# Index scores as two stacked fp32r passes, block 0 ranked by what it drops, a ranking round before the additions

## What is computed

```python
isc = relu(einsum('bqhd,bkd->bqhk', iq_block, ik))     # scores, 8 heads
isc = einsum('bqhk,bqh->bqk', isc, iw_block)           # weighted sum over heads
isc = where(allowed, isc, NEG)                         # keys of later chunks of 64 are not allowed
_, sel = top_k(isc, topk)                              # topk = 128
```

## Time and profile before

| what | value |
|---|---|
| median of three runs | 1713.42 us |
| the profiled execution | 1714.06 us, its span 1712.2 us |
| PE busy over the span | 1683.4 us, 98% |
| the projection's part of the span | up to about 233.5 us |
| PE in 12.0 to 232.3 us | 216.82 of 220.30 us |
| DVE / ACT / POOL in the same | 149.75 / 79.35 / 100.04 us |

### The profile page before, as it was taken

The page is one execution under the profiler, slowest core; times in us unless marked ns, Lnnn a source line. Parts: engine busy times, 40 slices in busy tenths (PEclk is TensorE's granted clock), DMA queues, the critical chain, the costliest instruction groups (busy, mean ns, idle before and its releaser), DMA issues.

```text
span 1712.2 us, 23324 instructions
## 1 busy us (share of the span) xinstructions
PE 1683.4 (98%) x7786; PEld 1381.9 (81%) x7786; DVE 1091.5 (64%) x2933; ACT 581.6 (34%) x916; POOL 937.8 (55%) x875
## 2 busy tenths in 40 slices
PE   9999999999999999999999999999999999999997
PEld 7877777788888888888888888888888888888886
DVE  4259966456788854444444444434788888888886
ACT  4333227243323222222222222224333333333333
POOL 2744415004433037777777777762777677767710
PEclk9999999999999999999999999999999999999999
DMA  5322142026669554444447444455999999999991
GB/s 177 106 62 62 50 88 62 15 99 222 240 231 315 162 154 143 142 146 147 148 155 235 147 141 144 146 162 190 387 390 369 370 371 363 376 374 368 362 331 49
DMA packets 182673, 351.03 MB, mean 205 GB/s; under 512 B 35600, under 2 KB 118928, under 8 KB 182448
## 3 DMA queue, kind: packets, MB, share of 16 engines
q1 hardware_dynamic: 117824, 255.47, 44.6%
q0 software_dynamic: 34816, 67.41, 11.0%
q10 hardware_dynamic: 29952, 27.28, 4.8%
HBM read 289.04 MB, written 61.02 MB: 204 GB/s over the span
## 4 chain that ended last, share of the span: by engine, by line
PE 74%; DVE 1%; DMA 1%; SPq 1%; POOL 0%; ACT 0%; issue 0%; DVEq 0%; POOLq 0%
PE psum L243 25%; PE psum L244 24%; PE psum L245 24%; DMA ts_raw_wq<-in_peer_wq 1%; PE psum L1735 1%; SPq L1700 0%; POOL ts_lo_wq L1578 0%; SPq L1567 0%; DVE ts_lo_u L1578 0%; POOL ts_lo_u L1578 0%; DVE hit L1867 0%; DVE mixed L2142 0%; DVE mixed L2119 0%; ACT ts_hi_wq L1573 0%; ACT ts_hi_u L1573 0%
## 5 line engine op out<-in xcount | busy, mean ns | idle before, releaser
L2336 POOL DMA_INDIRECT gate_map<-gate_total,gate_at x384 | 403.5, 1051 | 200.9 <-DVE same_expert L2073 110.2
L243 PE MATMUL psum<-x_hi,ts_hi_u 128*128 128x512 f32 x1024 | 399.1, 390 | 2.4 <-POOL ts_lo_u L1578 1.8
L244 PE MATMUL psum<-x_lo,ts_hi_u 128*128 128x512 f32 x1024 | 398.4, 389 | 0.0
L245 PE MATMUL psum<-x_hi,ts_lo_u 128*128 128x512 f32 x1024 | 398.4, 389 | 0.0
L1578 DVE TENSOR_TENSOR ts_lo_u<-ts_raw_u,ts_hi_u 128x1024 fp32r<-128x1024 f32 x116 | 142.2, 1226 | 336.6 <-ACT ts_hi_u L1573 336.6
L245 PE MATMUL psum<-v_hi,c_lo 128*128 128x512 f32 x768 | 298.8, 389 | 0.0
L243 PE MATMUL psum<-v_hi,c_hi 128*128 128x512 f32 x768 | 298.8, 389 | 0.0
L244 PE MATMUL psum<-v_lo,c_hi 128*128 128x512 f32 x768 | 298.8, 389 | 0.0
L1573 ACT ACTIVATE ts_hi_u<-ts_raw_u 128x1024 fp32r<-128x1024 f32 x128 | 135.4, 1058 | 395.0 <-PE psum L245 395.0
L2236 ACT ACTIVATE v_hi<-v_raw 128x1024 fp32r<-128x1024 f32 x128 | 135.8, 1061 | 313.8 <-PE psum L245 310.9
L243 PEld LDWEIGHTS psum<-x_hi,ts_hi_u 128*128 128x128 f32 x1024 | 192.2, 188 | 42.8 <-POOL ts_lo_u L1578 1.9
(11 more groups left out here) (264 smaller groups left out, 2296.0 us busy)
## 6 DMA issues: line engine op xcount, KB each, us to landing
ts_raw_u<-in_peer_u SPq DMA_DIRECT2D x128, 512.0 KB, 3.6
v_raw<-in_peer_v SPq DMA_DIRECT2D x128, 512.0 KB, 5.9
gate_map<-zeros SPq DMA_DIRECT2D x32, 768.0 KB, 6.5
act_in<-up_acts SPq DMA_DIRECT2D x128, 192.0 KB, 6.3
gate_in<-gate_map SPq DMA_DIRECT2D x128, 192.0 KB, 6.6
up_acts<-ut_out_u ACTq DMA_DIRECT2D x104, 192.0 KB, 1.9
raw_in<-in_w_in SPq DMA_DIRECT2D x56, 256.0 KB, 2.8
ts_raw_wq<-in_peer_wq SPq DMA_DIRECT2D x16, 512.0 KB, 6.5
```

What stands on the lines that cost most here:

```text
L243: nc.tensor.matmul(out, l_hi, r_hi, start=first, stop=False)
L244: nc.tensor.matmul(out, l_hi, r_lo, start=False, stop=False)
L245: return nc.tensor.matmul(out, l_lo, r_hi, start=False, stop=last)
L2336: nc.gpsimd.indirect_dma_start(gate_cells, bass.IndirectOffsetOnAxis(places["gate_at"][:, b, j:j + 1], 0), dn.total[:, b, j:j + 1], None). ...
```

## The change

1. **Index queries.** `iq_t` (fp32, two heads stacked) is replaced by `iq_a` and `iq_b` (four heads each, fp32r). Partitions 0 to 63 hold the high part of a head's 64 values, partitions 64 to 127 the low part of the same values. To get both, the rotated tile is written twice, once by POOL and once by DVE, side by side for each head (`rot_twice`, now in `mixed[:, 2 + n % 2]`), so a turn has 8 transposes into two banks. ACT copies both banks with rounding, then DVE subtracts the rounded values from PSUM in the lower half (`low_turned`).
2. **Index keys.** `ik_hi` holds the high part on both halves, `ik_lo` the low part on 64 partitions. A score is one fp32r pass on 128 rows (high and low query parts with the high keys) and one on 64 rows (high query part with the low keys).
3. **Waits.** The turn of rotated output n waits for `idx_lo_done` of n - 2 (n = 2 to 10); an `iq` turn waits for DVE's copy too; DVE's copy of n waits for the turn of n - 2.
4. **Block 0** is ranked by its 16 lowest keys: its weights `iw` are negated, its sums lie reversed in another part of its row, and 2 rounds find the 16 to leave out. The planner then has 50 rounds.
5. **A round first.** On DVE the first round of an output stands before the first two additions, if it ranks a block that is not being added.

```diff
-    iq_t = sb("iq_t", [P, IDX_HEADS // 2, FRAMES], c=c)
-    ik_t = sb("ik_t", [P, ROWS], c=c)
+    iq_a = sb("iq_a", [P, IDX_HEADS // 2, FRAMES], F32R, c=c)
+    iq_b = st["iq_b"]
+    ik_hi = sb("ik_hi", [P, ROWS], F32R, c=c)
+    ik_lo = st["ik_lo"][0:IDX_DIM]
...
+    IQ_BANKS = (4, 6)
+    DROPPED = key_width(0) - TOPK
+    def rounds_of(b):
+        return ROUNDS if b else DROPPED // 8
+    def rounds_ahead(i):
+        scored = [x for j, (x, _, _) in enumerate(items) if items_at(i) and j >= items_at(i)[0]]
+        return sum(order[q] not in scored for q, _ in rounds_at[i][:1])
+    SPLIT_TURNS = sum(name in ("iq", "misc") for _, name, _ in outs)
...
             # PE, turn
+                if 2 <= n < SPLIT_TURNS + 2:
+                    pe.wait_ge(idx_lo_done, n - 1)
+                if name == "iq":
+                    pe.wait_ge(rot_copied, n + 1)
+                    if n == 1:
+                        pe.wait_ge(mt_done, 1)
+                    for x in range(2):
+                        for t in range(4):
+                            last = nc.tensor.transpose(psum[:, IQ_BANKS[x] + n % 2, t * P:(t + 1) * P],
+                                                       rot_twice(n)[:, 4 * x + t].rearrange("p t d -> p (t d)"), ident[:])
+                    last.then_inc(rot_turned, 1)
+                    return
...
             # PE, index_scores
-                s = slice(IDX_DIM * (h % 2), IDX_DIM * (h % 2) + IDX_DIM)
-                nc.tensor.matmul(psum[:, 6 + j % 2, 0:w], iq_t[s, h // 2, b * P:(b + 1) * P],
-                                 ik_t[s, x * w:(x + 1) * w], start=True, stop=True).then_inc(idx_scored, 1)
+                parts = (iq_a, iq_b)[h // 4][:, h % 4, b * P:(b + 1) * P]
+                cols = slice(x * w, (x + 1) * w)
+                nc.tensor.matmul(psum[:, 6 + j % 2, 0:w], parts, ik_hi[:, cols], start=True, stop=False)
+                nc.tensor.matmul(psum[:, 6 + j % 2, 0:w], parts[0:IDX_DIM], ik_lo[:, cols], start=False, stop=True).then_inc(idx_scored, 1)
...
         # DVE, end of dve_rotate
+            if name == "iq":
+                dve.wait_ge(cos_done, n + 1)
+                if n >= 2:
+                    dve.wait_ge(rot_turned, n - 1)
+                nc.vector.tensor_tensor(rot_twice(n)[:, :, 1], by_head(t_cos, n), by_head(t_sin, n), ALU.add).then_inc(rot_copied, 1)
+        def low_turned(dve, i):
+            n = nrot[i]
+            _, name, b = outs[i]
+            dve.wait_ge(turned_copied, n + 1)
+            if name == "misc":
+                r, col = rows(b), META + b * P if b < NB else 0
+                last = nc.vector.tensor_tensor(ik_lo[:, col:col + r], psum[0:IDX_DIM, 4 + n % 2, P:P + r],
+                                               ik_hi[0:IDX_DIM, col:col + r].bitcast(F32), ALU.subtract)
+            else:
+                for x, dst in enumerate((iq_a, iq_b)):
+                    part = dst[IDX_DIM:P, :, b * P:(b + 1) * P]
+                    last = nc.vector.tensor_tensor(part, psum[IDX_DIM:P, IQ_BANKS[x] + n % 2, :].rearrange("p (h n) -> p h n", n=P),
+                                                   part.bitcast(F32), ALU.subtract)
+            last.then_inc(idx_lo_done, 1)
...
         # DVE, loop over outputs
             for i in range(len(outs)):
                 if i in nrot:
                     dve_rotate(dve, i)
+                for t in turns_after(i):
+                    if t in rotated[:SPLIT_TURNS]:
+                        low_turned(dve, t)
...
+                early = rounds_ahead(i)
+                for q, t in rounds_at[i][:early]:
+                    dve_round(dve, q, t)
                 for j in items_at(i)[:2]:
                     dve_add(dve, j)
-                for q, t in rounds_at[i]:
+                for q, t in rounds_at[i][early:]:
                     dve_round(dve, q, t)
...
         # POOL
+                elif name == "iq":
+                    nc.gpsimd.tensor_tensor(rot_twice(n)[:, :, 0], by_head(t_cos, n), by_head(t_sin, n), ALU.add).then_inc(rot_done, 1)
...
         # ACT, copy_turned
+                if name == "iq":
+                    for x, dst in enumerate((iq_a, iq_b)):
+                        last = nc.scalar.activation(dst[:, :, b * P:(b + 1) * P],
+                                                    psum[:, IQ_BANKS[x] + n % 2, :].rearrange("p (h n) -> p h n", n=P), ACT.Copy)
+                    last.then_inc(turned_copied, 1)
+                    return
```

More of the change, by code:

```diff
@@ L151, in program @@
             stream = ExitStack()
+            with ExitStack() as over_rq_t:
+                ik_lo = sb_high("ik_lo", [P, ROWS], F32R, c=over_rq_t)
             ret = dict(
@@ L161, in program @@
                 bias=sb("sel_bias", [P, NB, ROWS], c=stream),
-                gate=sb("gate", [P, NB, 512], c=stream),
+                ik_lo=ik_lo,
             )
+            with ExitStack() as over_gate:
+                st["iq_b"] = sb("iq_b", [P, IDX_HEADS // 2, FRAMES], F32R, c=over_gate)
+            st["gate"] = sb("gate", [P, NB, 512], c=stream)
             st.update(rq_t=ret["rq_t"], rk_t=ret["rk_t"], rv=ret["rv"])
@@ L391, in project @@
     turned_copied = sem("turned_copied")
+    idx_lo_done = sem("idx_lo_done")
+    rot_copied = sem("rot_copied")
+    IQ_BANKS = (4, 6)
     copied = sem("plain_copied")
@@ L408, in project, with ranked, placed @@
     ROUNDS = TOPK // 8
+    DROPPED = key_width(0) - TOPK
+    assert DROPPED % 8 == 0 and 0 < DROPPED < TOPK and order[-1] == 0
+    def rounds_of(b):
+        return ROUNDS if b else DROPPED // 8
+    def ranked(b):
+        w = key_width(b)
+        return bias[:, b, 0:w] if b else bias[:, 0, w:2 * w]
+    def placed(b, cols):
+        return ranked(b)[:, cols] if b else ranked(0)[:, ::-1][:, cols]
     ITEMS = 4
@@ L424, in project @@
     room = [0 if i < first_round or i + 1 == len(outs) else 2 if i in nrot else 3 for i in range(len(outs))]
-    work = sum(ROUNDS * cost(b) for b in range(NB))
+    work = sum(rounds_of(b) * cost(b) for b in range(NB))
     rounds_at, done, at = [[] for _ in outs], 0, first_round
     for q, b in enumerate(order):
-        for t in range(ROUNDS):
+        for t in range(rounds_of(b)):
             while done * sum(room) >= sum(room[:at + 1]) * work:
@@ L432, in project @@
             done += cost(b)
+    def rounds_ahead(i):
+        scored = [x for j, (x, _, _) in enumerate(items) if items_at(i) and j >= items_at(i)[0]]
+        return sum(order[q] not in scored for q, _ in rounds_at[i][:1])
+    SPLIT_TURNS = sum(name in ("iq", "misc") for _, name, _ in outs)
+    assert all(outs[i][1] in ("iq", "misc") for i in rotated[:SPLIT_TURNS])
     def rows(b):
@@ L631, in dve_round @@
             w = key_width(b)
-            r = bias[:, b, 0:w]
-            unseen = bias[0:CHUNK, b, w - CHUNK:w]
+            r = ranked(b)
+            unseen = placed(b, slice(w - CHUNK, w))[0:CHUNK]
             if t == 0:
                 dve.wait_ge(idx_added, max(j for j, it in enumerate(items) if it[0] == b) + 1)
-                nc.vector.memset(unseen, NEG).then_inc(masked_off, 1)
+                nc.vector.memset(unseen, NEG if b else -NEG).then_inc(masked_off, 1)
                 dve.wait_ge(masked_off, 2 * q + 1)
@@ L753, in copy_turned @@
                 else:
-                    tile, h0 = {"iq": (iq_t, 0), "dq0": (st["dq_t"], 0), "dq1": (st["dq_t"], 4), "rq": (st["rq_t"], 0)}[name]
+                    tile, h0 = {"dq0": (st["dq_t"], 0), "dq1": (st["dq_t"], 4), "rq": (st["rq_t"], 0)}[name]
                     dst = tile[:, h0:h0 + 4, b * P:(b + 1) * P]
```

25 lines of the change are left out of this document (16 added, 9 removed).

## The result

The changed kernel takes 1720.79 us (median of six runs; the kernel before beside it 1713.47), a ratio of 1.0039, interval 1.0028 to 1.0050: slower by 7.3 us, where 6.9 were forecast. A second set gave 1720.40 beside 1713.70, +6.7. The profiled execution took 1719.5 us, its span 1717.7. One of the six runs took 4024.54 us, and the ratio leaves it out.

What follows compares the result with a forecast made beforehand. TensorE (PE), busy 98% of the span, was taken as the bound: only what it executes or waits for in the projection counts. +1.9 + 5.0 + 0 = +6.9 us on 1713.42 gave 1720.3 us, 8-in-10 range 1713.2 to 1724.2.

Steps and rivals of the forecast that it cites:

- Part 1: Index scores on TensorE: 80 row-count changes at 0.2 us plus 10.0 of passes, 26.0 against 24.1 before, +1.9 us.
- The estimate: Alternative price for the scores' row changes from 166 ns fixed latency: 80 cost 13.3 us, scores -0.8, whole 1717.6; not adopted.
- Part 2: Turns of the index queries on TensorE: added transposes, two new waits and shared-port delay, +5.0 us (3.1 to 8.6).
- Transposes: In the four index-query turns: 16 more transposes at 0.108 us each, 1.7 us on TensorE.
- Stall before turn 2: TensorE waits for turn 0's low part, ready at 48.75 after a chain over DVE and ACT: 2.25 us.
- The second low part: After turn 2, TensorE waits again for turn 1's low part, ready at 49.95: another 0.35 us.
- the port's +0.5: In the turns, DVE's new SBUF additions may get stuck beside POOL on the shared port: +0.5 us, -1.4 to +4.1.
- the rounding: In the turns, transposes and stalls summed to 4.3 us and were rounded to 4.5.
- rival 2: POOL wins the shared port against DVE's additions: turns cost 8.0 instead of 5.0, total 1723.3 us; 17% chance.
- Part 3: The rest, such as fewer ranking rounds, the round first and small key operations: 0 us, as DVE ends nothing.
- Rival 1: Row count changes for free between a score's passes; the ReLU limits bursts, -6.5 us on scores, total 1711.9; 14% chance.
- Rival 3: Low parts are ready in time for the turns, together with Rival 1: 1.7 - 6.5 = -4.8, 1708.6 us; 5% chance.

Runs made afterwards that it cites:

- e1_rows128: Changed kernel, but each score's second pass also runs on 128 rows, low key parts on both halves: 1712.82 us.
- second trace: Profiled execution of the changed kernel, run again without any edit in a second set: median 1720.40 us.
- e3_reorder: Changed kernel, but at outputs 4 and 5 turned copies go ahead of plain copies and low parts ahead of the rotation: 1717.29 us.
- e2: Kernel before with the ranking edits alone (block 0 by its 16 left-out keys, a round first), scores and turns as before: 1713.54 us.
- e11: Changed kernel without the ranking round ahead of the first two additions, nothing else: 1719.60 us.
- e8: e4_both with ScalarE's ReLUs ahead of its turned copy, and index queries turned with four transposes as in the kernel before: 1707.10 us.
- e4_both: Changed kernel with the edits of both e1_rows128 and e3_reorder: 1709.28 us.
- e5_rows64: Changed kernel, but each score's first pass also runs on only 64 rows, leaving out low query parts with high keys: 1715.10 us.
- e9_rounds_last: e8 without the round ahead, all ranking rounds of an output again behind its first two additions: 1705.92 us.
- e10_best: e9_rounds_last, but at output 5 ScalarE copies the turned queries of blocks 2 and 3 ahead of two weight splits: 1705.01 us.

## Why the prediction was right

**Part 1 (+1.9 forecast).** The bursts grew by 25.42 - 21.87 = 3.55 us. The entry into a burst no longer changes the row count and is 0.17 us shorter (0.36 for 0.53, above), 11 times: 1.87. Net **+1.7**. Per change: 0.32 - 0.123 = 0.197 us for 264 columns; for 400, eight passes in 3.00 us are 0.375 each, less 0.180 (118.20 to 118.38 in e1_rows128) is 0.195. The forecast took 0.2 from a single burst's edges. That ReLU waits vanish at 0.64 us per score came true as well.

The Trainium skill's rule (TensorEngine Tiling (Array Packing), Key Properties: another tiling mode drains the engine) agrees in direction with the trace. The estimate from TensorE: Matmul & The Clock Gate (Single matmul latency), 166 ns each, would have been 0.03 us per change too low.

**Part 2 (+5.0).** Transposes: a pair of turns takes 1.66 us (41.20 to 42.86) instead of 0.79, twice: 1.74, forecast 1.7. Stall before turn 2: 2.30, forecast 2.25; the low part was ready at 48.76 (48.07 + 0.69), forecast 48.75, and PE began 0.26 later. The second low part: 2.03 for the second pair (49.02 to 51.05) less 1.66 is 0.37, forecast 0.35. Sum 4.4. The mis-sized term is the port's +0.5, with the rounding: it cost the chain nothing. DVE's two additions in the chain began 0.04 to 0.05 us ahead of POOL's and took 0.69; POOL's took 1.81 and 1.79 instead of the 1.3 of the earlier trace rows, and nobody waited for them. That also settles rival 2: DVE got in first both times. Ahead of the chain it was otherwise: the additions of blocks 0 and 1 stood beside POOL's weight splits and took 1.33 and 0.87 us (34.38 and 37.01), but PE waited for neither.

What this part does not have is the clock. In the second trace the stall is followed by a pair of turns at 1.2 GHz, and the part costs 1.35 us more (e3_reorder, above).

**Part 3 (0).** 0, by e2 and e11. The reason given, that PE asks for the banks an output later, was not the whole of it: in e8 the place of the round cost 1.3 us. That it costs nothing in the changed kernel because its scores are slow enough for the additions is argued from this; e8 differs from it in the order of the ReLUs and the turns as well.

**Sum.** 1.7 + 4.4 = 6.1, and the gate copy is 6.15 later, 0.12 of it there already at the first turn. The medians say 6.7 and 7.3, and the stages behind the barrier don't show the difference. The second trace does: with the fall of the clock it is 6.15 - 0.12 + 1.35 = 7.4 from the first turn on. In the first set the profiled execution, without the fall, is the shortest (1719.5); the four others in the ratio took 1720.57 to 1720.94, which a fall would explain but no trace of them shows. So the mechanisms held, and the number was in part luck: 0.8 too much, mostly for the port and the rounding, stood in for a cost of up to 1.35 that the prediction does not have.

**Rivals.** Rival 1 named the right lever: with row changes taken away (e1) the kernel is not slower than before, 1712.8 where 1711.9 was computed. Rival 3's combination is e4_both, 1709.3 against 1708.6. Both were refused for the right reason, what a change costs at the edges of a 64-row burst. The 0.33 us alone would not have shown it: behind four 128-row transposes the first 512-column pass of the kernel before also lasts 0.32 us (164.44 to 164.76), but there it starts early, as in the earlier trace rows. The 0.33 behind the 16-row turns, read without the start, is no evidence by itself.

## What to carry to other kernels

Look for places in the trace where TensorE's row count changes before splitting an operand into passes of different height: two passes of equal height with a superfluous product were cheaper by 0.2 us per pass than a pass that uses half of the rows. When a wait is added, write down all that the waited-for engine has queued ahead of it, and move that behind where it has time: plain copies, rotations and weight splits held up low parts here, and moves in an order took 2.1 us back in one place and 0.8 in another. Behind a new stall of TensorE look at the granted clock too, in more than one execution: in three of five the stall here came with a slower clock behind it, 1.35 us more. An order that is free now can cost when what hid it gets faster, so test it again in the final version.

## What the runs showed of the hardware

- A change between 128 and 64 rows costs 0.195 to 0.197 us, and the weight load does not run ahead across it; between passes of the same height, 128 or 64, it starts 0.11 to 0.13 us ahead (e1_rows128 and e5_rows64).
- Behind a stall of TensorE of 2.3 us the granted clock was 0.50 to 0.51 over the next 16 transposes in three of five profiled executions and 1.00 in two; behind stalls of 0.8 and 0.9 us (e9_rounds_last, e8_four_turns) it stayed at 1.00.
- Half the partitions were not cheaper here, and in e8_four_turns and e10_best the next operation came later. ScalarE's copies of 512 columns last 0.60 us on 128 partitions in the changed kernel and 0.59 on 64 in e10_best, but begin 0.48 us apart there (46.34 to 46.82) and 0.59 here. VectorE's subtractions on 64 partitions last 0.69 us in both kernels, but begin 0.61 us apart where the results stay in their half (47.46 to 48.07) and 0.69 where they go to the other (e8_four_turns: 42.43 to 43.12). ScalarE's copies in e10_best:

```profile
46.59 0.58 ACT L824 ACTIVATE iq_a<-psum 64x512 fp32r<-64x512 f32 x1
47.18 0.59 ACT L824 ACTIVATE iq_b<-psum 64x512 fp32r<-64x512 f32 x1
```

For VectorE the height is 64 in both kernels, so what is left is that the result goes to the other half or that the halves alternate. For ScalarE, whether the half, its change from one operation to the next or the height does this was not tried.
